# RMS factors in mid first phase, x scaled from its pieces, four waits moved, and index keys with 72 columns moving, in a hybrid attention layer

## The reference

```python
xn = x * rsqrt(mean(x * x) + EPS) * norm_g          # RMS norm, per token
h  = xn @ w_in                                      # one projection, split among all branches
qi, ki, wi = ...                                    # index queries (8 x 64), index key (64), head weights (8)
qi = rope(qi);  ki = rope(rms_norm(ki, idx_k_norm_g))
score = sum_h relu(qi_h . ki) * wi_h                # picks the keys of mixer A (top-k)
A = sparse softmax attention;  B = stick-breaking attention
y = x + (sigmoid(ga) * W_a[A * silu(ua)] + sigmoid(gb) * W_b[B * silu(ub)]) @ w_o
```

## Time and profile before

| | |
|---|---|
| median of 3 runs | 554.64 us (553.42 to 559.67) |
| profiled execution | 554.89 us, of it span 553.1 us |
| PE busy | 530.0 us, 96% (4344 matmuls, and 4344 weight loads) |
| DVE / ACT / POOL busy | 328.7 / 229.5 / 76.1 us |
| DMA | 50.45 MB, 91 GB/s over the span |

### The profile page before, as it was taken

The page is one execution under the profiler, slowest core; times in us unless marked ns, Lnnn a source line. Parts: engine busy times, 40 slices in busy tenths (PEclk is TensorE's granted clock), DMA queues, the critical chain, the costliest instruction groups (busy, mean ns, idle before and its releaser), DMA issues.

```text
span 553.1 us, 10275 instructions
## 1 busy us (share of the span) xinstructions
PE 530.0 (96%) x4344; PEld 501.8 (91%) x4344; DVE 328.7 (59%) x662; ACT 229.5 (41%) x387; POOL 76.1 (14%) x75
## 2 busy tenths in 40 slices
PE   6959899999999999999999899999999999999998
PEld 5748899999989899999998788889899999999997
DVE  5965667899959998586821567653332432256231
ACT  6715556634255436554334665643421332222110
POOL 3410400003212333275000000000000000000000
PEclk9979999999999999999999999999999999999999
DMA  8531021332332422022130005021113321247311
GB/s 327 208 127 40 0 87 30 129 116 81 113 117 78 158 77 77 1 78 97 61 122 28 1 8 200 2 77 39 52 65 115 114 78 42 74 149 272 119 40 52
DMA packets 15358, 50.45 MB, mean 91 GB/s; under 512 B 2416, under 2 KB 5872, under 8 KB 11728
## 3 DMA queue, kind: packets, MB, share of 16 engines
q1 hardware_dynamic: 15168, 49.79, 25.6%
q10 hardware_dynamic: 144, 0.00, 0.0%
HBM read 42.82 MB, written 6.82 MB: 90 GB/s over the span
## 4 chain that ended last, share of the span: by engine, by line
PE 86%; DVE 6%; ACT 3%; issue 2%; DMA 1%; POOL 1%; SPq 0%; ACTq 0%
PE PS L564 36%; PE PS L773 13%; PE PS L834 9%; PE PS L816 8%; PE PS L687 4%; PE PS L666 3%; PE PS L548 2%; PE PS L642 2%; PE PS L609 2%; DVE wlo L1184 2%; PE PS L503 2%; PE PS L751 2%; DMA stage<-in_x_kw_qi 1%; PE PS L589 1%; DVE flo L1192 1%
## 5 line engine op out<-in xcount | busy, mean ns | idle before, releaser
L1184 DVE TENSOR_TENSOR wlo<-raw,whi 128x2048 fp32r<-128x2048 f32 (+1 forms) x36 | 75.7, 2104 | 59.1 <-ACT whi L880 59.1
L564 PE MATMUL PS<-xhi,whi 128*128 128x272 f32 x320 | 94.6, 296 | 0.2 <-ACT bias_r L955 0.2
L564 PE MATMUL PS<-xlo,whi 128*128 128x272 f32 x320 | 92.4, 289 | 0.0
L564 PE MATMUL PS<-xhi,wlo 128*128 128x272 f32 x320 | 92.1, 288 | 0.0
L880 ACT ACTIVATE whi<-raw 128x2048 fp32r<-128x2048 f32 (+1 forms) x36 | 61.6, 1713 | 51.7 <-PE PS L773 33.5
L564 PE MATMUL PS<-whi,xhi 128*128 128x256 f32 x256 | 73.6, 287 | 2.8 <-ACT vals L950 2.8
L564 PE MATMUL PS<-wlo,xhi 128*128 128x256 f32 x256 | 72.3, 282 | 0.0
L564 PE MATMUL PS<-whi,xlo 128*128 128x256 f32 x256 | 71.9, 281 | 0.0
L564 PEld LDWEIGHTS PS<-xhi,whi 128*128 128x128 f32 x320 | 60.2, 188 | 4.0 <-issue 3.7
L564 PEld LDWEIGHTS PS<-xhi,wlo 128*128 128x128 f32 x320 | 60.3, 188 | 0.0
L564 PEld LDWEIGHTS PS<-xlo,whi 128*128 128x128 f32 x320 | 60.2, 188 | 0.0
(11 more groups left out here) (230 smaller groups left out, 1152.9 us busy)
## 6 DMA issues: line engine op xcount, KB each, us to landing
raw<-in_w_units SPq DMA_DIRECT2D x28, 1024.0 KB, 4.9
raw<-in_w_mixes SPq DMA_DIRECT2D x8, 512.0 KB, 3.5
stage<-in_x_kw_qi SPq DMA_DIRECT2D x7, 564.0 KB, 8.8
res<-in_x_kw_qi SPq DMA_DIRECT2D x1, 2176.0 KB, 8.0
out<-res SPq DMA_DIRECT2D x16, 136.0 KB, 1.7
out<-vals SPq DMA_DIRECT2D x2, 1024.0 KB, 6.2
out<-kT SPq DMA_DIRECT2D x1, 1088.0 KB, 9.5
out<-tm SPq DMA_DIRECT2D x1, 1024.0 KB, 7.3
```

Of the source, the lines that this page charges most:

```text
L564: mm = pe.matmul(out, lhsT, rhs, start=(k == 0), stop=(k == 23))
L1184: dve.tensor_tensor(wlo[:, uu % 2, 0:n], raw[:, uu % 2, 0:n], whi[:, uu % 2, 0:n].bitcast(F32), ALU.subtract).then_inc(w_lo, 1)
```

## The change

The diff has these parts. The gain norm_g no longer comes by a DMA of its own but as one more column of each x chunk. DVE in place of ACT makes the first high part of the index columns. In the first phase the 72 key columns now move and tokens are stationary: behind each matmul of 512 query columns stands one of 72 key columns with the same stationary tile, all in bank 7; the transposes go, and ACT scales the key rows straight out of PSUM, ahead of the queries. The means are made before the weight remainders of vb0 and vb1; POOL's powers go in one instruction; the factors of the sample go with the others. x is scaled as x times gain times rB in one step, in place, all 544 tokens. POOL does the keys' root ahead of the sample's query sum. Of later waits: gate0's weight parts are made in turn 2 of the softmax stage, gate2's last half stands after the last weighing, and out0's weight parts are made before the seventh m split.

```diff
-                for h in range(2):
-                    for k, (a, b) in enumerate(PASSES):
-                        mm = pe.matmul(ps[0:KW, 6 + h, 0:HALF_NT], fpart[b][:, c, 0:KW], xpart[a][:, c, halved(h)],
-                                       start=False, stop=(c == KC - 1 and k == 2))
-                    if c == KC - 1:
-                        mm.then_inc(kw_done, 1)
                 for t, (t0, n) in enumerate(TILES[0:4]):
                     for k, (a, b) in enumerate(PASSES):
-                        mm = pe.matmul(ps[:, t, :], xpart[a][:, c, t0:t0 + n], fpart[b][:, c, KW:FIRST],
-                                       start=False, stop=(c == KC - 1 and k == 2))
+                        pe.matmul(ps[:, t, :], xpart[a][:, c, t0:t0 + n], fpart[b][:, c, KW:FIRST],
+                                  start=False, stop=(c == KC - 1 and k == 2))
+                        mm = pe.matmul(ps[:, 7, KW * t:KW * t + KW], xpart[a][:, c, t0:t0 + n], fpart[b][:, c, 0:KW],
+                                       start=False, stop=(c == KC - 1 and k == 2), skip_group_check=True)
                     if c == KC - 1:
                         mm.then_inc(qi_done, 1)
                 pe.wait_ge(x_st, c + 1)
                 for b in range(2):
-                    mm = pe.matmul(ps[0:2 * DEC, 4, :], xst[:, c, :], fpart[b][:, c, KW:FIRST],
-                                   start=False, stop=(c == KC - 1 and b == 1))
+                    pe.matmul(ps[0:2 * DEC, 4, :], xst[:, c, :], fpart[b][:, c, KW:FIRST],
+                              start=False, stop=(c == KC - 1 and b == 1))
+                    mm = pe.matmul(ps[0:2 * DEC, 7, KW * 4:KW * 5], xst[:, c, :], fpart[b][:, c, 0:KW],
+                                   start=False, stop=(c == KC - 1 and b == 1), skip_group_check=True)
...
                     pe.wait_ge(r_wide_ready, 1)
                     for t in range(4):
-                        last = pe.matmul(ps[:, 5, P * t:P * t + P], r_wide[:, t, :], ident, start=True, stop=True)
-                    last.then_inc(rb_done, 1)
-                if c == 5:
-                    pe.wait_ge(rb_out, 1)
-                    pe.matmul(ps[:, 5, 0:DEC], r_wide[0:DEC, 4, :], ident[0:DEC, 0:DEC], start=True,
+                        pe.matmul(ps[:, 6, P * t:P * t + P], r_wide[:, t, :], ident, start=True, stop=True)
+                    pe.matmul(ps[:, 5, DEC:2 * DEC], r_wide[0:DEC, 4, :], ident[0:DEC, 0:DEC], start=True,
                               stop=True).then_inc(rb_done, 1)
...
-            pe.wait_ge(kw_raw_out, 2)
-            pe.wait_ge(rb_out, 2)
-            for t, (t0, n) in enumerate(TILES):
-                last = pe.transpose(ps[0:n, 5, KW * t:KW * t + KW], kw_raw[:, t0:t0 + n], ident[0:KW, 0:KW])
-            last.then_inc(kw_tr, 1)
+            pe.wait_ge(rb_out, 1)
             for g in groups_of("vb0"):
+                if g == 1:
+
+                    pe.wait_ge(kw_out, 1)
                 group(g)
...
                 if t == N_STEPS + 1:
-                    gate(EARLY_GATES, 1)
+                    gate(EARLY_GATES, 1, (0,))
                 if t >= 2:
                     if t == N_STEPS + 1:
                         pe.wait_ge(sample_rows, sample_units("va1"))
                     if t == 8:
                         group_out_wait(pe, LAST_GROUP[U["va1"]])
                     weigh_pair(t - 2, probT, pt_out, av_out, av_done)
+            gate(EARLY_GATES, 1, (1,))
...
-                if c == 0:
-                    act.wait_ge(f_in, 16)
-                act.activation(fhi[:, c, :], stage(c)[:, NT:CHUNK_COLS], ACT.Copy).then_inc(f_hi, 1)
+                act.activation(xhi[:, c, :], x_of(c), ACT.Copy, scale=gain_of(c)).then_inc(x_hi, 1)
+                if c >= 1:
+                    act.activation(fhi[:, c, :], first_of(c), ACT.Copy).then_inc(f_hi, 1)
...
+                act.activation(xhi[:, c, :], x_of(c), ACT.Copy).then_inc(xn_hi, 1)
+
+            for c in range(KC):
                 normed_high(c)
-            for h in range(2):
-                act.wait_ge(kw_done, h + 1)
-                act.activation(kw_raw[:, halved(h)], ps[0:KW, 6 + h, 0:HALF_NT], ACT.Copy).then_inc(kw_raw_out, 1)
-            normed_high(KC - 1)
-            act.wait_ge(xs_scaled, KC + 1)
-            act.activation(xhi[:, :, SEQ:NT], xs[:, :, SEQ:NT], ACT.Copy).then_inc(xn_hi, 1)
             act.wait_ge(x_rs, 1)
+
+            act.wait_ge(xn_lo, 4)
             for t, (t0, n) in enumerate(TILES):
                 act.wait_ge(qi_done, t + 1)
                 if t == 4:
+                    act.activation(kw_low, ps[DEC:2 * DEC, 7, KW * t:KW * t + KW], ACT.Copy, scale=xrs[DEC:2 * DEC, 4:5])
+                last = act.activation(tm[0:n, t, W:W + KW], ps[0:n, 7, KW * t:KW * t + KW], ACT.Copy, scale=xrs[0:n, t:t + 1])
+            last.then_inc(kw_out, 1)
+            for t, (t0, n) in enumerate(TILES):
+                if t == 4:
                     act.activation(qi_low, ps[DEC:2 * DEC, 4, :], ACT.Copy, scale=xrs[DEC:2 * DEC, 4:5])
                 act.activation(tm[0:n, t, 0:W], ps[0:n, t, :], ACT.Copy, scale=xrs[0:n, t:t + 1]).then_inc(qi_out, 1)
-                if t == 3:
-                    act.wait_ge(kw_tr, 1)
-                    for tt, (t0, n) in enumerate(TILES):
-                        last = act.activation(tm[0:n, tt, W:W + KW], ps[0:n, 5, KW * tt:KW * tt + KW], ACT.Copy,
-                                              scale=xrs[0:n, tt:tt + 1])
-                    last.then_inc(kw_out, 1)
...
-                if t == 0:
+                if t == 2:
                     unit_next(POST_B[-1])
...
+                if d == 6:
+                    w_high("out0")
                 act.wait_ge(mixed, d + 1)
                 act.activation(mhi[:, d, :], summed[:, d % 2, :], ACT.Copy).then_inc(m_hi, 1)
                 if d + 1 <= 5:
                     w_high(f"mix{d + 1}")
                 elif d == 5:
                     w_high("mix7")
-                elif d == 6:
-                    w_high("out0")
-                else:
+                elif d == 7:
                     w_high("out1")
...
+                if c == 0:
+                    dve.wait_ge(f_in, 16)
+                    dve.tensor_copy(fhi[:, 0, :], first_of(0)).then_inc(f_hi0, 1)
...
             dve.tensor_copy(x_sum[:, NT:NT + DEC], x_sum[:, SEQ:NT]).then_inc(x_added, 1)
+            dve.wait_ge(x_ss, 1)
+            dve.wait_ge(const_ready, 4)
+            dve.tensor_scalar(xss[:, 0:4], ps[:, 5, 0:8:2], 1.0 / D, EPS, ALU.mult, ALU.add)
+            dve.tensor_scalar(xss[0:2 * DEC, 4:5], ps[0:2 * DEC, 5, 8:9], 1.0 / D, EPS, ALU.mult, ALU.add).then_inc(x_mean, 1)
             w_low("vb0")
             w_low("vb1")
-
-            dve.wait_ge(x_sq, KC)
-            for c in range(KC):
-                last = dve.tensor_tensor(xs[:, c, :], xhi[:, c, :].bitcast(F32), xlo[:, c, :].bitcast(F32), ALU.add)
-            last.then_inc(x_whole, 1)
-            dve.wait_ge(x_ss, 1)
-            dve.tensor_scalar(xss[:, 0:4], ps[:, 5, 0:8:2], 1.0 / D, EPS, ALU.mult, ALU.add)
-            dve.tensor_scalar(xss[0:2 * DEC, 4:5], ps[0:2 * DEC, 5, 8:9], 1.0 / D, EPS, ALU.mult, ALU.add).then_inc(x_mean, 1)
             dve.wait_ge(rb_done, 1)
-            dve.tensor_copy(rB[:, 0:SEQ], ps[:, 5, :]).then_inc(rb_out, 1)
-            dve.wait_ge(x_whole, 1)
+            dve.tensor_copy(rB[:, 0:SEQ], ps[:, 6, :])
+            dve.tensor_copy(rB[:, SEQ:NT], ps[:, 5, DEC:2 * DEC]).then_inc(rb_out, 1)
             dve.wait_ge(rb_out, 1)
 
             def scaled(c):
-                dve.tensor_tensor(xs[:, c, 0:SEQ], xs[:, c, 0:SEQ], rB[:, 0:SEQ], ALU.mult).then_inc(xs_scaled, 1)
-
-            def normed_low(c):
-                dve.wait_ge(xn_hi, c + 1)
-                dve.tensor_tensor(xlo[:, c, 0:SEQ], xs[:, c, 0:SEQ], xhi[:, c, 0:SEQ].bitcast(F32),
-                                  ALU.subtract).then_inc(xn_lo, 1)
+
+                dve.scalar_tensor_tensor(x_of(c), x_of(c), gain_of(c), rB, ALU.mult, ALU.mult).then_inc(xs_scaled, 1)
...
             scaled(0)
             for c in range(KC):
                 if c + 1 < KC:
                     scaled(c + 1)
-                if c == 5:
-                    dve.wait_ge(rb_done, 2)
-                    dve.tensor_copy(rB[:, SEQ:NT], ps[:, 5, 0:DEC]).then_inc(rb_out, 1)
-                if c == KC - 1:
-                    dve.wait_ge(rb_out, 2)
-                    wide = rB[:, SEQ:NT].unsqueeze(1).to_broadcast([P, KC, DEC])
-                    dve.tensor_tensor(xs[:, :, SEQ:NT], xs[:, :, SEQ:NT], wide, ALU.mult).then_inc(xs_scaled, 1)
-                normed_low(c)
-            dve.wait_ge(xn_hi, KC + 1)
-            dve.tensor_tensor(xlo[:, :, SEQ:NT], xs[:, :, SEQ:NT], xhi[:, :, SEQ:NT].bitcast(F32),
-                              ALU.subtract).then_inc(xn_lo, 1)
+                dve.wait_ge(xn_hi, c + 1)
+                dve.tensor_tensor(xlo[:, c, :], x_of(c), xhi[:, c, :].bitcast(F32), ALU.subtract).then_inc(xn_lo, 1)
```

(57 more changed lines are left out.)

54 lines of the change are left out of this document (25 added, 29 removed).

## The result

The changed kernel takes 554.2 us (median of 20 runs, 551.30 to 556.49) beside 557.11 us for the kernel before (median of 20, 553.42 to 560.31). The ratio is 0.995, with a 95% interval of 0.9928 to 0.9973: half a per cent faster, which counts as no change, where 1.2 to 1.3% was forecast and 541.5 to 552.5 us was the range. The profiled execution took 554.61 us with a span of 552.8; that of before 554.89 and 553.1.

The account below looks back on a forecast made before the run. TensorE, busy 96% of the span, bounds the kernel, so only its standing still or slow running can be won. Gains 3.9 + 0.8 + 0.3 + 1.1 + 1.1 = 7.2 us from 554.89 give 547.7 us, range 541.5 to 552.5.

Parts of the forecast that it names:

- Step (a): First phase, broadcast of the RMS factors: means ahead of the weight remainders on DVE, so PE's 6.7 us wait goes.
- Step (b): First phase, behind the factors' wait: with no hole, no second start at the lower clock, 2.0 us gained.
- the clock falls inside the first phase: Rival, first phase: grant falls to 1.2 GHz, each 4.7 us chunk costs 4.7 us more; 566 us with four; chance 0.04.
- Step (d): First-phase keys: fourteen 72-column matmuls cost 0.67 us more a chunk, 4.7 over seven chunks; first chunk 0.5 us lost.
- loads hide: Rival, first-phase keys: a small matmul costs only its columns, 0.04 us; 542.0 us; chance 0.13.
- plain fp32 pace: Rival, first-phase keys: 72 columns take 0.146 us each, 4.8 us worse in all; 552.5 us; chance 0.12.
- load exposed: Rival, first-phase keys: weight load fully exposed at 0.19 us, 1.12 us a chunk worse than assumed; 556.7 us; chance 0.04.
- Keys' way to the dots: Index transposes: PE's 1.7 us wait goes, 0.7 comes back at vb1 and 0.2 at vb0's bank; net 0.8 us.
- The other moves: Later moved waits: gate0's weights gain 0.3 us, gate 2's second half 1.1, out0's remainder 1.1.

Follow-up runs that it names:

- experiment 1: Changed kernel with VectorE's remainders of vb0 and vb1 ahead of its wait for the column sums instead of behind the means: 548.72 us, ratio to before 0.9873.
- experiment 4: Changed kernel with eight more 512-column matmuls, results overwritten, where PE waits for the factors: 551.73 us, ratio to before 0.9903.
- experiment 7: Changed kernel with 272-column keys, vb0's remainder ahead of the means and vb1's behind POOL's copies: 542.64 us, ratio to before 0.9746.
- experiment 6: Changed kernel with the remainders of vb0 and vb1 first and the keys back to 272 moving columns: 543.87 us, ratio to before 0.9769.

## Why the prediction failed, step by step

**Step (a), the factors: wrong, and the cause of the miss.** "POOL's part took 35.22 - 32.72 = 2.5 us and chunk 4 on PE takes over 4 us, so PE meets the factors without a wait." The 2.5 us are from the earlier trace rows, where DVE was idle, and were carried to a place where the same change puts DVE's two remainders right beside them. There the power alone takes 5.36 us and POOL's part 6.3 (28.59 to 34.92). Chunk 4 covered it until 33.05, and 1.87 were left. The prediction looked at DVE's order for what is queued behind its wait, found the remainders not urgent, and did not ask whom they disturb. With the remainders elsewhere (experiment 1) the step holds. The trace of before had the price further on: two powers of eight columns take 3.24 us together at 247.85, with no weight remainder beside them, and 5.30 where the first stands beside one (`wlo`), which is itself held up there, 3.97 us instead of 2.27.

```profile
238.04 3.97 DVE L1184 TENSOR_TENSOR wlo<-raw,whi 128x2048 fp32r<-128x2048 f32 x1
239.83 5.30 POOL L1678 TENSOR_TENSOR nrs<-nss,halves 128x8 f32<-128x8 f32 x2
...
247.85 3.24 POOL L1678 TENSOR_TENSOR nrs<-nss,halves 128x8 f32<-128x8 f32 x2
```

**Step (b), no second low clock: wrong, for the same reason.** The clock fell after the 1.87 us in the profiled run, and the broadcast and chunk 5 took 0.9 and 2.3 us more than at the full pace; by the lists of clocks it falls in some runs and not in others. The rival "the clock falls inside the first phase" was priced at 4.7 us a chunk, with PE's 72-column matmuls as the cause; here it came behind a wait, went with that wait in experiments 1 and 4, and cost one chunk 2.3 us.

**Step (d), the keys: right in size, short in the first chunk.** Chunks take 4.68 to 4.72 us, forecast 4.7. That undoing them brings 6.1 us, where the prediction counted 4.7 + 0.5 - 0.4 = 4.8 for them, is mostly the first chunk: 7.03 us in experiment 1 beside 5.59 in experiment 7 (5.09 to 10.68), 1.4 where 0.5 was counted. The low pace at the start, taken over from before at 3.3 us, lasted longer in every trace with pairs. The rivals "loads hide", "plain fp32 pace" and "load exposed" are out (theirs would have been chunks of 3.8, 5.3 and 5.8 us); 0.11 us for an uncovered load, from the earlier trace rows, was the right row.

**Keys' way to the dots: right.** No wait at the index transposes; 0.45 us at vb0's first bank, when PE asks for it again (forecast 0.2), and 0.90 at bank 7 (0.7): net 0.4 instead of 0.8.

**The other moves: right.** 0.54 and 1.79 us in the softmax turns (forecast 0.5 and 1.9), and both waits of 1.1 us gone. Together 2.6 us where 2.5 was forecast.

**The sum.** Between the profiled executions the span fell by 0.3 us (553.1 to 552.8) where 7.2 was forecast. With (a) made true (experiment 1) it falls by 6.4, to 546.7, and the median is 548.7 us (forecast 547.7), inside the range; most of what is left is the first chunk. The terms other than (a), (b) and the first chunk that the traces show were sized within half a microsecond.

## What to carry to other kernels

A duration read from a trace belongs to what ran beside it: before an operation of GpSimd is moved, look at what VectorE will do at that moment, and keep VectorE instructions with two SBUF inputs out of it, whole runs of them: the power here did not slip in between two, nor between eight. A wait of TensorE costs more than its length when the clock falls behind it (here 1.87 us and some 3 more), so the best place for these remainders was the idle time of their own engine ahead of the critical step, not behind it. And a matmul with few moving columns cost a weight load of 0.11 us here, with 2 columns as with 72; turned so that 272 columns move, the same keys were 6 us cheaper in all, transposes and the shorter low pace at the start included.

## What was not expected of the hardware

- Back-to-back VectorE subtractions with two SBUF inputs kept a GpSimd power waiting across two instructions (5.36 us) and across eight (5.77 us), until 1.04 us after the last; alone it takes 1.18. A cast of 32 columns, 0.42 us otherwise, was kept for 0.70 us and no longer.
- A wait of 1.87 us on TensorE was followed by the lower clock, another of 2.29 us was not; with none or one of 0.78 us (experiments 1, 4 and 6) the granted clock read 1.00 there. In the changed kernel it fell when TensorE had already gone on, and stayed down for some 7 us.
- At the start, pairs of 512 and 72 columns stayed at the low pace for 5.0 to 10.1 us, other orders for 3.1 to 4.7.
